# RWKV-7 and gated-delta trunk: shift of the next group inside the inverse, stacked chunk operands, alternating PSUM buffers, gate matrices on ScalarE

## What is computed

```python
def rwkv7_scan(r, decay, k, v, kk, a):
    def step(S, inp):
        r_t, w_t, k_t, v_t, kk_t, a_t = inp
        s_kk = jnp.einsum('bhij,bhj->bhi', S, kk_t)
        S = (S * w_t[:, :, None, :] - s_kk[..., None] * (kk_t * a_t)[:, :, None, :]
             + v_t[..., None] * k_t[:, :, None, :])
        return S, jnp.einsum('bhij,bhj->bhi', S, r_t)
...
def gated_delta_rule_chunked(q, k, v, g, beta):
    gc = jnp.cumsum(g, axis=-1)
    decay = jnp.exp(jnp.where(lower, gc[..., :, None] - gc[..., None, :], -jnp.inf))
    kkt = jnp.einsum('bhncd,bhnsd->bhncs', k_beta, k) * decay
    tri = jnp.where(strict, kkt, 0.0) + jnp.eye(GDN_CHUNK, dtype=kkt.dtype)
    sol = lax.linalg.triangular_solve(tri, rhs, left_side=True, lower=True, unit_diagonal=True)
```

## Time and profile before

| | us |
|---|---|
| median of 3 runs | 3143.51 (3138.36 to 3145.25) |
| the profiled execution | 3143.37 |
| its span in the trace | 3141.7 |

### The profile page before, as it was taken

How to read it: one execution, slowest core, us unless ns; L and a number is a source line. 1 busy time by engine, 2 the same in 40 slices (tenths; PEclk the granted TensorE clock), 3 DMA queues, 4 the chain that set the end, 5 groups by cost and what they waited for, 6 DMA issues and landing times.

```text
span 3141.7 us, 57226 instructions
## 1 busy us (share of the span) xinstructions
PE 2992.0 (95%) x22276; PEld 2617.4 (83%) x22276; DVE 1819.8 (58%) x2422; ACT 1421.3 (45%) x2121; POOL 13.1 (0%) x28
## 2 busy tenths in 40 slices
PE   8899998989999999999999999999998999999997
PEld 8777877778888888889898887899877888888886
DVE  4555555475455555565666666566567645555555
ACT  4443344334343444434555655455554434444442
POOL 0000000000000000000000000000000000000000
PEclk9999999999999999999999999999999999999999
DMA  6333333455555555544333334443335555555553
GB/s 227 99 100 101 98 100 121 148 201 194 188 188 189 195 193 192 191 159 140 112 127 127 123 121 141 160 149 122 111 126 186 197 194 188 191 188 190 189 188 113
DMA packets 156997, 492.08 MB, mean 157 GB/s; under 512 B 15584, under 2 KB 50528, under 8 KB 155776
## 3 DMA queue, kind: packets, MB, share of 16 engines
q1 hardware_dynamic: 154032, 476.18, 45.0%
q0 software_dynamic: 2224, 11.89, 1.0%
q10 hardware_dynamic: 544, 1.05, 0.1%
HBM read 486.96 MB, written 2.10 MB: 156 GB/s over the span
## 4 chain that ended last, share of the span: by engine, by line
PE 79%; DVE 10%; ACT 5%; issue 4%; DVEq 0%; DMA 0%; ACTq 0%; SPq 0%
PE pp L415 35%; PE mp L415 11%; PE pp L399 8%; PE mp L399 8%; PE pp L401 4%; PE mp L401 4%; DVE wl L1313 2%; DVE ws L1663 2%; ACT wh L870 1%; PE mp L798 1%; PE mp L762 1%; PE mp L746 1%; PE mp L738 1%; PE mp L804 1%; ACT ws L1131 0%
## 5 line engine op out<-in xcount | busy, mean ns | idle before, releaser
L1313 DVE TENSOR_TENSOR wl<-raw,wh 128x1024 fp32r<-128x1024 f32 (+1 forms) x936 | 1102.1, 1185 | 912.3 <-ACT wh L870 907.4
L870 ACT CAST wh<-raw 128x1024 fp32r<-128x1024 f32 (+1 forms) x936 | 944.3, 1019 | 878.4 <-PE pp L415 308.1
L415 PE MATMUL pp<-aT,wh 128*128 128x256 f32 x4704 | 906.0, 293 | 37.7 <-DVE wl L1313 21.2
L415 PEld LDWEIGHTS pp<-aT,wh 128*128 128x128 f32 x4704 | 738.8, 193 | 59.2 <-DVE wl L1313 23.4
L415 PE MATMUL pp<-aT,wl 128*128 128x256 f32 x2352 | 668.7, 284 | 0.0
L415 PEld LDWEIGHTS pp<-aT,wl 128*128 128x128 f32 x2352 | 454.0, 193 | 0.0
L415 PE MATMUL pp<-wh,hTh 128*128 128x512 f32 x896 | 360.9, 403 | 17.2 <-DVE hTl L1693 7.8
L399 PE MATMUL pp<-aT,wh 128*128 128x512 f32 x1024 | 363.0, 399 | 0.2 <-issue 0.2
L399 PE MATMUL mp<-aT,wh 128*128 128x512 f32 x1024 | 359.1, 396 | 0.0
L415 PE MATMUL pp<-wh,hTl 128*128 128x512 f32 x896 | 351.5, 392 | 0.0
L415 PE MATMUL pp<-wl,hTh 128*128 128x512 f32 x896 | 351.0, 392 | 0.0
(11 more groups left out here) (298 smaller groups left out, 2662.2 us busy)
## 6 DMA issues: line engine op xcount, KB each, us to landing
raw<-in_w_dram SPq DMA_DIRECT2D x800, 512.0 KB, 3.3
raw<-in_w_dram SPq DMA_DIRECT2D x136, 384.0 KB, 3.5
ws<-in_ln_dram POOLq DMA_DIRECT2D x8, 1024.0 KB, 7.5
out_dram<-xres SPq DMA_DIRECT2D x8, 256.0 KB, 2.0
ws<-in_lora_dram POOLq DMA_DIRECT2D x8, 192.0 KB, 2.6
xres<-in_x_dram ACTq DMA_DIRECT2D x2, 512.0 KB, 6.0
xres<-in_x_dram SPq DMA_DIRECT2D x2, 512.0 KB, 6.7
ws<-in_c_dram POOLq DMA_DIRECT2D x1, 768.0 KB, 7.4
```

The source lines that it names most:

```text
L415: last = mm(o, lhs, rhs, start=opens and m == 0, stop=end and kk == 1 and m == 2, skip_group_check=True)
L870: nc.scalar.copy(wh[:, q % RING, :, 0:width], raw[:, q, :, 0:width]).then_inc(S("hi_ready"), 1)
L1313: tt(wl[:, q % RING, :, 0:width], raw[:, q, :, 0:width], f(wh[:, q % RING, :, 0:width]), ALU.subtract).then_inc(S("lo_ready"), 1)
```

## The change

RWKV. (1) VectorE's token shift is cut into seven pieces and done one group ahead, in the later steps of the inverse, the first one at the end of the LoRA stage. (2) In step 1 the scores and the transposes of v come ahead of LoRA. (3) The mask is added to the scores first; ScalarE's Abs reads the masked scores; the decay's constant goes into an exponential's bias; signs change accordingly, and two products on VectorE go. (4) b is stored turned by one chunk, so that b and k of a chunk, and u and v, lie on the two halves of the partitions: `BK`, `UV`, `GM`. The state's update is one matmul of 128 rows instead of two of 64, y's products with the gram matrices one of 128x128 instead of four of 64x64, and y's product with the state is done twice. ScalarE copies the transposes in six pieces. (5) `HOPS0` changes: half units of the 32 per step were 3, 3, 3, 2, 3, none in steps 5, 11, 16, 22 and 27, else one; they are 1, 3, 2, 2, 3, none in steps 21 and 23, else one.

Gated-delta. (6) The PSUM buffers alternate from group to group, with `lag` at its usual 2; two groups stand in the loop's body. (7) The eight gate matrices are formed by ScalarE in step 4 instead of VectorE in step 0. (8) The mean square doesn't wait for each of its four parts. (9) The last `o_scale` stands in step 29 instead of 28, behind that step's units.

```diff
-HOPS0 = (3, 4, 3, 3, 3) + 23 * (1,)
+HOPS0 = (1, 3, 2, 2, 3) + 16 * (1,) + (0, 1, 0, 1, 1, 1, 1)
...
+        btr = lay(T)
+        BK, UV = (r2(lay(4 * P), a=4) for _ in range(2))
+        tokw = r2(lay(2 * P), a=2)
...
+                pe.wait_ge(S("evacuated"), 2 * m + (2 + P_GROUPS0 + 2))
+                nc.tensor.transpose(mb[2][:, 0:P], sbq[:, 2, 0:P], ident)
+                nc.tensor.transpose(mb[2][:, P:T], sbq[:, 2, P:T], ident)
+                mm(mb[3][:, 0:T], sbq[:, 1, 0:P], sbq[:, 0, :], start=True, stop=True, skip_group_check=True)
+                mm(mb[3][:, T:T + P], sbq[:, 1, P:T], sbq[:, 0, P:T], start=True, stop=True,
+                   skip_group_check=True).then_inc(S("scores"), 1)
+
                 pe.wait_ge(S("lora_in"), 16 * m1)
-
                 pe.wait_ge(S("rw_o"), m1)
...
                 to_tiles()
+                turned = lambda n: slice((n + 3) % 4 * HC, (n + 3) % 4 * HC + HC)
                 for t in range(TT):
-                    for w, src in enumerate((bt, kt_)):
+                    for w in range(2):
                         for h, hf in QUADS:
-                            at = slice(t * P + HC * hf, t * P + HC * hf + HC)
-                            last = mm(mb[h][half(hf), (2 * t + w) * P:(2 * t + w + 1) * P], src[half(h), at],
-                                      KR[half(h), hf, :, t, :], start=t + w == 0, stop=True, skip_group_check=True)
+                            n, e = 2 * t + hf, 1 - hf
+                            src = kt_[half(h), n * HC:(n + 1) * HC] if w else btr[half(h), turned(n)]
+                            last = mm(mb[h][half(hf if w else e), n * P:(n + 1) * P], src, KR[half(h), hf, :, t, :],
+                                      start=t + w == 0, stop=True, skip_group_check=True)
                 last.then_inc(S("gram"), 1)
...
+                for t in range(TT):
+                    at = slice(t * P, (t + 1) * P)
+                    for bank, q, src in ((0, t, rkv[:, 2, at]), (0, 2 + t, KR[:, t, 0, :, :].rearrange("p t c -> p (t c)")),
+                                         (1, 2 * t, kt_[:, at]), (1, 2 * t + 1, btr[:, at])):
+                        last = nc.tensor.transpose(mb[bank][:, q * P:(q + 1) * P], src, ident)
                 last.then_inc(S("tokT"), 1)
...
+                to_tiles()
+                a_times_x(1)
+                pe.wait_ge(S("tok_ready"), 2 * m + 1)
...
-                for c in range(4):
-                    t, hf = divmod(c, 2)
-                    R = slice(64 * hf, 64 * hf + 64)
-                    st_in, yc_ = (Sb, Sa)[c % 2], slice(64 * c, 64 * c + 64)
-                    if c:
-                        pe.wait_ge(S("state0"), 3 * m + c)
-                        mm(mb[0][R, 0:P], KR[:, hf, 0, t, :], st_in, start=True, stop=True,
-                           skip_group_check=True).then_inc(S("u_psum"), 1)
+                for n in range(4):
+                    t, hf = divmod(n, 2)
+                    st_in, y_ = (Sb, Sa)[n % 2], mb[2][:, n * P:(n + 1) * P]
+                    if n:
+                        pe.wait_ge(S("state0"), 3 * m + n)
+                        if n < 3:
+
+                            last = mm(mb[0][:, 0:P], KR[:, hf, 0, :, :].rearrange("p t c -> p (t c)"), st_in, start=True, stop=True,
+                                      skip_group_check=True)
+                        else:
+                            last = mm(mb[0][half(1 - hf), 0:P], KR[:, hf, 0, t, :], st_in, start=True, stop=True,
+                                      skip_group_check=True)
+                        last.then_inc(S("u_psum"), 1)
                         yield
-                    if c == 0:
+                    if n == 0:
 
                         pe.wait_ge(S("WT_ready"), m1)
-                    pe.wait_ge(S("U"), 4 * m + c + 1)
-                    if c < 3:
-                        mm(mb[3][:, 0:P], tok[R, 0, t, :], U[R, :], start=True, stop=False, skip_group_check=True)
-                        mm(mb[3][:, 0:P], tok[R, 1, t, :], tok[R, 2, t, :], start=False, stop=True,
+                    pe.wait_ge(S("U"), 4 * m + n + 1)
+                    if n < 3:
+                        mm(mb[3][:, 0:P], BK[:, n, :], UV[:, n, :], start=True, stop=True,
                            skip_group_check=True).then_inc(S("dS"), 1)
-                    if c:
-                        mm(mb[2][:, yc_], st_in, KR[:, hf, 1, t, :], start=True, stop=False, skip_group_check=True)
-                    for h in range(2):
-                        hs = slice(64 * h, 64 * h + 64)
-                        mm(mb[2][hs, yc_], U[R, hs], GM[R, t, h, 0, 1, :], start=c == 0, stop=False, skip_group_check=True)
-                        last = mm(mb[2][hs, yc_], tok[R, 2, t, hs], GM[R, t, h, 1, 1, :], start=False, stop=True,
-                                  skip_group_check=True)
-                    last.then_inc(S("y_psum"), 1)
+                    if n:
+                        for h in range(2):
+                            mm(y_[:, half(h)], st_in, KR[:, hf, 1, t, :], start=h == 0, stop=False, skip_group_check=True)
+                    mm(y_, UV[:, n, :], GM[:, n, :, 1, :], start=n == 0, stop=True,
+                       skip_group_check=True).then_inc(S("y_psum"), 1)
...
-            drive(group1(P_L1, B_L1), 3 * UNITS, 0, then(new_x(2), gates()), HOPS_GATES)
-            with pe.Fori(1, 5) as i:
-                drive(group1(i * 3 + P_L1, i * 3 + B_L1), 3 * UNITS, 0, mix1(i - 1), HOPS1)
+            def group1(n, b, par):
+                return blocks(n, b, "B", A, (par, 1 - par, par), WIDE)
+
+            drive(group1(P_L1, B_L1, 0), 3 * UNITS, 0, then(new_x(2), gates()), HOPS_GATES)
+            with pe.Fori(0, 2) as i:
+                drive(group1(i * 6 + (P_L1 + 3), i * 6 + (B_L1 + 3), 1), 3 * UNITS, 0, mix1(i * 2), HOPS1)
+                drive(group1(i * 6 + (P_L1 + 6), i * 6 + (B_L1 + 6), 0), 3 * UNITS, 0, mix1(i * 2 + 1), HOPS1)
 
...
-                act.wait_ge(S("scores"), m1)
+                act.wait_ge(S("sb_masked"), m1)
+                st(go(sbb, sbc, ACT.Abs))
+                act.wait_ge(S("lora_used"), m1 + 1)
                 st(go(ew[:, 0:T], mb[0][:, 0:T], ACT.Exp, scale=-1.0, bias=nprm[:, bass.ds(m, 1), 0]))
                 go(ew[:, T:2 * T], mb[1][:, 0:T], ACT.Exp, scale=-1.0,
                    bias=nprm[:, bass.ds(m, 1), 1]).then_inc(S("gates_exp"), 1)
-                nc.scalar.copy(vtk, r2(mb[1][:, T:2 * T], a=TT)).then_inc(S("vtk"), 1)
-
-                st(go(sbb, mb[3][:, 0:384], ACT.Abs))
-
-                act.wait_ge(S("kk0"), m1)
+                act.wait_ge(S("shifted"), 2 * m1)
                 go(ksq, kk0, ACT.Square).then_inc(S("ksq"), 1)
                 st.settle()
                 st(go(sbb, sbb, ACT.Exp, scale=-1.0))
                 st.settle()
                 go(sbb, sbb, ACT.Ln, bias=1.0).then_inc(S("softplus"), 1)
+                act.wait_ge(S("scores"), m1)
+                nc.scalar.copy(vtk, r2(mb[2][:, 0:T], a=TT)).then_inc(S("vtk"), 1)
...
-                st(nc.scalar.copy(tok[:, 0:2, :, :], mb[0][:, :].rearrange("p (w t c) -> p w t c", w=2, t=TT)))
-                nc.scalar.copy(tok[:, 2:4, :, :], mb[1][:, :].rearrange("p (w t c) -> p w t c", w=2, t=TT)).then_inc(S("tok_ready"), 1)
+                for i in range(2):
+                    st(nc.scalar.copy(UV[half(i), :, :].rearrange("p (t f) c -> p t f c", f=2)[:, :, i, :],
+                                      r2(mb[0][half(i), 0:T], a=TT)))
+                nc.scalar.copy(tokw, r2(mb[0][:, T:2 * T], a=2)).then_inc(S("tok_ready"), 1)
+                st(nc.scalar.copy(BK[half(0), :, :], r2(mb[1][half(0), :], a=4)))
+                st(nc.scalar.copy(BK[half(1), 1:4, :], r2(mb[1][half(1), 0:3 * P], a=3)))
+                nc.scalar.copy(BK[half(1), 0, :], mb[1][half(1), 3 * P:4 * P]).then_inc(S("tok_ready"), 1)
...
-                        go(sqj, os[c][:, h, :], ACT.Square, accum_out=oss[:, h:h + 1]).then_inc(S("oss"), 1)
-                        act.wait_ge(S("oss"), 8 * g + (4 * c + h + 1))
+                        st(go(XTc[:, h, :, :].rearrange("p f c -> p (f c)"), os[c][:, h, :], ACT.Square, accum_out=oss[:, h:h + 1]))
+                    st.settle()
...
+                for c in range(TT):
+                    for h in range(4):
+                        last = go(UTg[:, c, h, :], UT, ACT.Copy, scale=head(gv, c, h))
+                        if c * 4 + h < 7:
+                            st(last)
+                last.then_inc(S("utg"), 1)
...
-                    nc.scalar.copy(zs, r2(pp[0][:, :], a=4)).then_inc(S("evacuated"), 1)
+                    nc.scalar.copy(zs, r2(pp[par][:, :], a=4)).then_inc(S("evacuated"), 1)
...
+                    yield
+                for _ in shift(0):
+                    pass
+                yield
+
+            def shift(m):
+
+                par = lambda j: prm[:, bass.ds(m, 1), j]
+                dve.wait_ge(S("evacuated"), m * 2 + (P_GROUPS0 + 3))
```

(63 more changed lines are left out.)

## The result

| | median, us | runs |
|---|---|---|
| before | 3144.29 (3138.36 to 3149.38) | 20 |
| after | 3151.29 (3143.72 to 3156.27) | 20 |

The ratio is 1.0018, 95% interval 1.0011 to 1.0024: the change makes the kernel slower, by 7 us between the medians. The forecast was 3129 us. The profiled execution of the changed kernel took 3154.0 us, with a span of 3152.3.

What follows compares the result with a forecast made beforehand. TensorE bounds the kernel, its matmuls busy 2992.0 of 3141.7 us, so only its work or waits can go. RWKV -20, gated-delta +3 and clock +3 make -14 us: from 3143.5 to 3129 us, range 3107 to 3147.

Steps and rivals of the forecast that it cites:

- the walk to attention: RWKV pass, chain from variance matmul to attention through ScalarE and VectorE: 19.2 us instead of 20.75, -1.55 us.
- Step 1: RWKV, variance matmul to start of scores: 5.35 us, with a new 2.3 us wait for the q, k, v copy.
- step 2: RWKV, from the start of the scores to the gates' exponentials: 3.0 us instead of 3.16.
- step 3: RWKV, from the gates' exponentials to the attention matmul: 10.85 us instead of 13.49.
- Rival B: The RWKV chain to attention gains nothing: RWKV only -6 us, gated-delta +4, total 3141 us; chance 0.2.
- From gram to variance: RWKV, gram matmuls to the next variance matmul, 39.9 us before: -0.65 us from covered waits, stacked operands and new waits.
- the term of the clock, +3: Halved clock (0.50) after TensorE's two new waits in each RWKV pass: +3 us in total.
- 14 waits: RWKV waits of about 2.3 and 2.0 us a pass, each given 1 in 4 for low clock, 1.0 us net.
- rival C: The two new waits of each RWKV pass drop the clock every time: slower, 3151 us; chance 0.1.
- gated-delta, +0.5 a boundary and +3 in all: Gated-delta: +0.5 us at four mixer-to-mixer boundaries, +0.9 at three output panels, -1 once; +4, or +3 with the clock.
- the z wait only moved: Gated-delta boundaries: the 13.7 us of z waits go, but the z copy-convolution-sigmoid chain ends last, so TensorE waits at L702.
- rival A: The z wait is a plain gain: gated-delta boundaries -11 us, perhaps -3 more by the clock, total 3112 us; chance 0.2.

Runs made afterwards that it cites:

- a_oscale28: The changed kernel with one edit undone, the last `o_scale` back in step 28 ahead of that step's weight splits: 3132.9 us, ratio 0.9968 to before.
- buf_only: The kernel before with the alternating PSUM buffers alone (two groups in the loop's body): 3141.3 us, ratio 0.9993 to before.

## Why the prediction was wrong, step by step

**Right: the walk to attention.** In the pass of after whose clock is 1.00 there, the variance matmul starts at 128.37, the scores at 133.75, the exponentials at 136.91 and the attention at 147.60:

```profile
128.37 0.70 PE L639 MATMUL mp<-ws 128*128 128x256 f32 x2
...
133.75 0.33 PE L484 MATMUL mp<-cc,ws 128*128 128x128 f32 x1 [2.55 <-ACT ws L1051]
...
147.60 0.70 PE L510 MATMUL mp<-ws 128*128 128x256 f32 x2 [1.85 <-ACT ws L968]
```

```profile
136.91 0.48 ACT L939 ACTIVATE ws<-mp,ws 128x256 f32<-128x256 f32 x1 [0.46 <-PE mp L496]
```

Step 1 is 5.38 (forecast 5.35), step 2 3.16 (3.0), step 3 10.69 (10.85), together 19.23 (19.2). The first attention stands at 85.0 (84.6), the pass is 62.6 (62.5). Rival B, that this chain gains nothing, is out. The shift in seven pieces cost nothing that shows. From gram to variance the wait at L572 was 1.7 us and not 0.5, but other waits went that I had kept, and the sum held.

**Wrong: the term of the clock, +3.** This is the step that failed first. The forecast gave each of 14 waits 1 in 4 and 1.0 us net. Measured: 11 pieces more in RWKV up to 530 us at 1.5 us each, **+16**. Three errors are in it. The chance: waits of 2.5 us were followed by 0.50 in 24 of 25 (the 1.8 us at L510 in 3 of 14, no more than the 1 in 4). The number of places: L572 was not among the 14, and 4 of its 7 waits had it. And the net price: I let part of the loss vanish in the wait on the way to attention; but LoRA and the scores are on that very chain. In the pass with the low clock scores to exponentials took 4.71 us instead of 3.16 (199.24 to 203.95), and the attention stood at 20.77 us, where it had stood before the change. The sample of the earlier trace rows, one fall in two, was too small (the whole trace of before has 5 in 7 in gated-delta), and I then set the chance below it because the new waits were shorter. The Trainium skill ("TensorE: Matmul & The Clock Gate", Why this matters for your kernels) warns of idle gaps between bursts; the runs here bear it out for gaps shorter than the one it names, with 2.5 us nearly always in RWKV and 1.7 us often. That was rival C in place and mechanism, to which I had given 0.1. That its 3151 us is the measured time is luck: it had 24 us for the clock in RWKV, where 16 were lost, and 4 for gated-delta, where it was 14.

**Wrong: gated-delta, +0.5 a boundary and +3 in all.** The transposes came 2.9 us later than before, counted from the o matmuls, which start at 1555.27 in the trace of before (the earlier trace rows give the rest: 5.49, now 8.37; forecast 2.7). The next step failed: the z copy was to be 1.1 us late and was 1.69 (9.25 to 10.94), since the half unit between them now runs where the clock is 0.50 (1562.3, behind the 3.0 us wait). The tap then was to regain 0.6 from the gate matrices that left VectorE; it regained 0.53, and now waits for ScalarE's product (0.52 in its row). So +1.16 instead of +0.5 at the first tap (13.52 to 14.68), and a pass of 105.0 to 105.2 us instead of 103.8. And I priced the edit only against before: the alternating buffers had opened room that `o_scale` at its old step would have used, as `a_oscale28` shows with 103.5 us a pass, and 102.6 instead of 105.4 near the end. The move alone is 1.7 us a pass and 2.5 to 2.8 in the last ones. Nor did the low clock go with the z wait: from 1480 to 2400 us it is 9 pieces instead of 5, some of them behind the new waits of 3.0 us. The last group pays for the move as well, in front of its output panel:

```profile
2385.69 1.11 PE L831 MATMUL mp<-cc,ws 128*128 128x128 f32 x4 [3.14 <-DVE ws L1717]
```

One more term was put at nothing: the loop body of two groups. The second pass is 4.2 to 4.4 us longer than its neighbours in the trace of after, and 3.4 in `buf_only`. Over the whole second layer `a_oscale28` needs 16.0 us less than the change and 2.2 less than before (1032.3, 1048.3 and 1034.5 us).

**Right or nothing:** the z wait only moved (rival A is out); the gate matrices on ScalarE cost tenths at most. The Trainium skill ("ScalarE: Activation LUTs", What ACT_TABLE_LOAD costs) gives 186 ns, 0.833 ns a column and some 93 ns for a scale by pointer. For 128 columns that makes an estimate of 386 ns; the trace agrees with 392 ns median, and 2.46 us for eight lies within the 1.7 to 3.2 of the prediction.

**The sum again.** Without the two terms the forecast was -20, all of it in RWKV; the kernel without most of the two causes measured -17. Its trace has 14.3 us less in the first layer, with three pieces of low clock more than before, which at 1.5 us each makes 19, and 4.3 less in the second layer, which was not in the forecast (the buffers alone, in `buf_only`, have 2.7 less there). So the gain of RWKV was sized right; that the total comes near the forecast's 3129 is luck in part. The two deductions were 3 and 3 us and should have been some 16 and 14.

**Open.** The first MLP, whose code is the same in all fourteen kernels, took 718.8 us in before, 721.7 in the change and up to 724.6 in `buf_only`; the second 731.0 to 741.0. One more piece of low clock at 644 us explains 1.5 of the change's 2.9; the rest is scatter of single executions whose cause isn't shown, and a difference of a few us between two traces means nothing unless it is tied to a place. Open too are the waits by "issue".

## What to carry to other kernels

Price a wait on TensorE by more than its length: in these traces low clock followed 2.1 us in half of the cases, 2.5 us nearly always in RWKV and about 3 us in 10 of 14 in gated-delta, so where a wait is that long, or stands close to another, count the low clock behind it as the likely case, and place it on whatever chain follows. Before a step is moved behind other work, ask what the same step would be worth at its old place in the *new* kernel, since another edit may just have made room. Units that can stand anywhere are best spent to split the longest wait, and each move wants a look at where the next-longest wait grows: one unit moved from the inverse to the scores cost 20 us by the ratios and 25 by the medians. And look at the "issue" rows of the waits, and at where they stand, before a loss is put down to the edit next to them.

## What the runs showed of the hardware

Low clock was recorded in pieces of 3.41 us, each worth 1.5 us of a stream of 256-column fp32 matmuls. Waits of 1.1 to 1.4 us with no other near were followed by it in 0 of 59 cases, waits of 2.5 us in 24 of 25, all in the RWKV part. It can settle into a rhythm: with a wait of 2.86 us in each pass, three passes in a row took 68.2 to 68.3 us with the same four pieces in each. And more matmuls can make a stretch shorter: with five and three useless ones in two waits of each pass, six passes took 379 us instead of 389. Where the two-group body of the gated-delta loop starts over, TensorE paused for 2.64 and 2.35 us and ScalarE for 1.93, while queue 14 (kind "instruction") moved 32 KB; that the one caused the other isn't shown.
